# Another order of the same instructions in the attention pairs of a one-core YOCO decode step

## What is computed

```python
def stick_breaking(q, k, v, bias, q_pos, k_pos):
    z = jnp.einsum('bthd,bshd->bhts', q, k).astype(jnp.float32) * (HEAD_DIM ** -0.5) \
        + bias.astype(jnp.float32)[None, :, None, None]
    causal = k_pos[None, :] < q_pos[:, None]
    log_beta = jax.nn.log_sigmoid(z)
    log_rest = jnp.where(causal, jax.nn.log_sigmoid(-z), 0.0)
    after = lax.cumsum(log_rest, axis=3, reverse=True) - log_rest
    a = jnp.where(causal, jnp.exp(log_beta + after), 0.0)
    out = jnp.einsum('bhts,bshd->bthd', a, v.astype(jnp.float32))
```

## Time and profile before

| what | us |
|---|---|
| median of 3 runs | 2781.6 |
| the profiled execution, device time | 2782.98 |
| its span, first to last instruction | 2781.3 |
| PE busy over the span | 2681.6 (96%) |
| DVE busy | 1327.5 (48%) |
| ACT busy | 763.3 (27%) |
| POOL busy | 1008.4 (36%) |
| mean granted clock of PE | 0.978 |

### The profile page before, as it was taken

One profiled execution on the slowest core, in us unless ns is written; L12 is line 12 of the kernel. 1 busy time (PEld: TensorE's weight loads), 2 busy tenths in 40 slices (PEclk: granted clock), 3 DMA queues, 4 the chain that ended last, 5 costly groups with the idle time before them and its releaser, 6 DMA issues.

```text
span 2781.3 us, 42516 instructions
## 1 busy us (share of the span) xinstructions
PE 2681.6 (96%) x16785; PEld 2564.6 (92%) x16785; DVE 1327.5 (48%) x1343; ACT 763.3 (27%) x1096; POOL 1008.4 (36%) x534
## 2 busy tenths in 40 slices
PE   7999999999999999999999999969999999999997
PEld 6989999999999999988888888749999999999997
DVE  5244453333333333678878878782533333333335
ACT  5112110000000000367767767661200000000003
POOL 4643475667676777000000000020433333333330
PEclk8999999999999999999999999879999999999998
DMA  3111133333333333423222222222211111111111
GB/s 116 46 39 32 45 91 95 115 114 115 114 115 114 114 114 118 165 66 100 82 74 79 83 86 83 93 101 86 61 46 46 47 46 47 46 47 46 40 38 63
DMA packets 247794, 220.18 MB, mean 79 GB/s; under 512 B 12842, under 2 KB 211298, under 8 KB 247586
## 3 DMA queue, kind: packets, MB, share of 16 engines
q1 hardware_dynamic: 229090, 206.75, 23.8%
q10 hardware_dynamic: 18496, 10.49, 1.3%
HBM read 162.42 MB, written 54.77 MB: 78 GB/s over the span
## 4 chain that ended last, share of the span: by engine, by line
PE 90%; DVE 5%; ACT 2%; issue 2%; ACTq 0%; DMA 0%; SPq 0%; DVEq 0%
PE ps L762 50%; PE ps L891 18%; PE aux L1021 8%; PE ps L973 3%; PE ps L946 2%; PE ps L928 2%; PE ps L958 2%; PE aux L992 1%; DVE scratch L1686 1%; PE aux L1027 1%; DVE v_all L1714 1%; PE aux L981 1%; PE aux L1061 0%; PE ps L842 0%; DVE sp_part_odd L1841 0%
## 5 line engine op out<-in xcount | busy, mean ns | idle before, releaser
L644 POOL TENSOR_TENSOR w_hi<-w_raw,ones_col 128x1024 fp32r<-128x1024 f32 x140 | 270.9, 1935 | 821.5 <-PE ps L762 536.6
L651 POOL TENSOR_TENSOR w_lo<-w_raw,w_hi 128x1024 fp32r<-128x1024 f32 x156 | 436.0, 2795 | 12.2
L762 PE MATMUL ps<-near_hi,w_hi 128*128 128x352 f32 x1632 | 357.7, 327 | 15.7 <-DVE near_lo L1673 12.1
L762 PE MATMUL ps<-near_lo,w_hi 128*128 128x352 f32 x1632 | 354.5, 325 | 0.0
L762 PE MATMUL ps<-near_hi,w_lo 128*128 128x352 f32 x1632 | 352.5, 324 | 0.0
L762 PEld LDWEIGHTS ps<-near_hi,w_hi 128*128 128x128 f32 x1632 | 279.3, 190 | 20.0 <-issue 12.0
L762 PE MATMUL ps<-in_hi,w_hi 128*128 128x352 f32 x1320 | 286.9, 325 | 3.7 <-issue 3.7
L1800 DVE TENSOR_TENSOR h<-h,ps 128x1056 f32<-128x1056 f32 x160 | 200.1, 1251 | 188.0 <-PE ps L891 187.8
L762 PE MATMUL ps<-in_lo,w_hi 128*128 128x352 f32 x1320 | 285.5, 324 | 0.0
L762 PE MATMUL ps<-in_hi,w_lo 128*128 128x352 f32 x1320 | 284.3, 323 | 0.0
L718 POOL TENSOR_TENSOR in_lo<-o_back,in_hi 128x1056 fp32r<-128x1056 f32 x7 | 18.1, 2589 | 732.6 <-ACT in_hi L1254 732.6
(11 more groups left out here) (229 smaller groups left out, 4373.6 us busy)
## 6 DMA issues: line engine op xcount, KB each, us to landing
w_raw<-in_w_gate_dram SPq DMA_DIRECT2D x44, 512.0 KB, 4.4
w_raw<-in_w_up_dram SPq DMA_DIRECT2D x44, 512.0 KB, 4.0
w_raw<-in_w_down_dram SPq DMA_DIRECT2D x44, 512.0 KB, 3.8
kept_hi<-pre_hi SPq DMA_DIRECT2D x64, 256.0 KB, 2.1
kept_lo<-pre_lo SPq DMA_DIRECT2D x64, 256.0 KB, 2.7
w_hi<-kept_hi SPq DMA_DIRECT2D x32, 512.0 KB, 3.7
w_lo<-kept_lo SPq DMA_DIRECT2D x32, 512.0 KB, 4.6
w_raw<-in_a_w_in_dram SPq DMA_DIRECT2D x16, 512.0 KB, 3.9
```

What stands on the lines that cost most here:

```text
L644: gp.tensor_tensor(hi, raw, one, ALU.mult).then_inc(w_hi_done, 1)
L651: gp.tensor_tensor(lo, raw, as32(hi), ALU.subtract).then_inc(w_ready, 1)
L762: last = mm(out[:, c, 0:CH], w[:, ks], x[:, k, c * CH:c * CH + CH], start=(k == 0 and n == 0), stop=(k == KT - 1 and n == 2))
```

## The change

In the four functions `pair` the calls stand in another order. No call is added or dropped, and X_ORDER is unchanged; AUX_LAST and X_LAST only name lists that were written out before. The core of the diff, from the first chunk on PE to the last:

```diff
@@ SP @@
                 if more:
-                    for n in (1, 2):
-                        slab(r + n, r_of + n, (r_of + n) % 2, chunk_done, 9 * p + 3 + 3 * n)
+                    slab(r + 1, r_of + 1, (r_of + 1) % 2, chunk_done, 9 * p + 6)
+                if more:
                     v_pages(p + 1, p + 1)
+                if more:
+                    slab(r + 2, r_of + 2, (r_of + 2) % 2, chunk_done, 9 * p + 9)
@@ PE, head of the pair @@
                 if past:
-                    values(q, o, 9)
+                    take_later(q, o, 10)
                 if more:
                     x_turn(p, c, ("c", 0), more)
                 if past:
+                    values(q, o, 9)
                     carry(q, o, 10)
                 if now:
+                    sample_start(p, c)
+                    x_turn(p, c, ("p", 0), more)
                     scores(p, c, 1)
-                    x_turn(p, c, ("p", 0), more)
...
+                    sample_scores(p, c, 0)
+                    x_turn(p, c, ("p", 1), more)
                     carry(p, c, 0)
                     scores(p, c, 3)
-                    x_turn(p, c, ("p", 1), more)
@@ PE, steps 6 to 11 @@
                 if now:
                     take_later(p, c, 6)
+                    scores(p, c, 8)
                     values(p, c, 5)
-                    scores(p, c, 8)
+                    sample_later(p, c)
                     carry(p, c, 6)
+                    scores(p, c, 9)
+                    take_later(p, c, 7)
+                    values(p, c, 6)
+                    sample_values(p, c)
+                    scores(p, c, 10)
                 if more:
                     x_turn(p, c, ("c", 7), more)
...
+                if more:
+                    x_turn(p, c, ("c", 8), more)
+                if now:
                     take_later(p, c, 9)
-                    scores(p, c, 11)
+                    values(p, c, 8)
                 if more:
                     x_turn(p, c, ("v", 1), more)
                 if now:
-                    values(p, c, 8)
+                    sample_turned(p, c)
                     carry(p, c, 9)
-                    sample_values(p, c)
                 if more:
                     x_turn(p, c, ("v", 2), more)
-                if now:
-                    take_later(p, c, 10)
-                    sample_turned(p, c)
@@ ACT, head @@
                 if now:
                     act.wait_ge(bias_done, p + 1)
+                    biased(p, c, 0)
+                    v_high(p, 1)
                 if past:
                     weights(q, o, 10)
                 if now:
-                    biased(p, c, 0)
+                    turned(p, c, ("p", 0), more)
                     exp_part(p, c, 0)
@@ ACT, end @@
                 if now:
+                    exp_part(p, c, 11)
                     weights(p, c, 9)
-                    sample_rows(p)
-                if more:
-                    turned(p, c, ("v", 2), more)
-                if now:
-                    exp_part(p, c, 11)
                     log_part(p, c, 11)
@@ DVE, steps 6 and 7 @@
                     logits(p, c, 5)
                     softplus(p, c, 6)
+                    capped(p, c, 7)
                     softplus_high(p, c, 6)
+                    a_low(p, c, 5)
+                    sample_capped(p)
                     softplus_low(p, c, 6)
-                    a_low(p, c, 5)
-                    capped(p, c, 7)
-                    sample_capped(p)
...
+                    softplus(p, c, 7)
+                    sample_softplus(p)
                     logits(p, c, 6)
@@ DVE, end of the pair @@
                     a_low(p, c, 8)
+                    softplus_high(p, c, 10)
+                    out(p, 1)
+                if more:
+                    chunk_evicted(p, c, 8)
+                if now:
                     logits(p, c, 9)
-                    out(p, 1)
-                    softplus(p, c, 10)
-                    softplus_high(p, c, 10)
                     softplus_low(p, c, 10)
```

More of the change, by code:

```diff
@@ L1000, in x_turn @@
             def x_turn(p, c, item, more):
-                order = X_ORDER if more else [x for x in X_ORDER if x[0] == "p"]
+                order = X_ORDER if more else X_LAST
                 at = order.index(item)
@@ L1114, in pair @@
                 if now:
+                    scores(p, c, 4)
+                    carry(p, c, 1)
+                    x_turn(p, c, ("p", 2), more)
+                    values(p, c, 1)
                     take_later(p, c, 2)
[L1116 to L1120, removed]
                 if more:
@@ L1123, in pair @@
                 if now:
-                    take_later(p, c, 3)
+                    carry(p, c, 2)
+                    scores(p, c, 5)
                 if more:
@@ L1127, in pair @@
                 if now:
-                    scores(p, c, 5)
+                    take_later(p, c, 3)
                     values(p, c, 2)
-                    carry(p, c, 3)
                 if more:
@@ L1156, in pair @@
                 if now:
-                    take_later(p, c, 7)
+                    take_later(p, c, 8)
+                    values(p, c, 7)
                 if more:
@@ L1160, in pair @@
                 if now:
-                    values(p, c, 6)
-                    scores(p, c, 9)
+                    scores(p, c, 11)
+                    carry(p, c, 8)
                 if more:
@@ L1574, in pair @@
                     weights(p, c, 5)
+                if more:
+                    k_high(p, c, 5)
+                if now:
                     exp_part(p, c, 7)
@@ L2016, in pair @@
                     softplus(p, c, 6)
+                    capped(p, c, 7)
                     softplus_high(p, c, 6)
+                    a_low(p, c, 5)
+                    sample_capped(p)
                     softplus_low(p, c, 6)
-                    a_low(p, c, 5)
-                    capped(p, c, 7)
-                    sample_capped(p)
+                    softplus(p, c, 7)
+                    sample_softplus(p)
+                    logits(p, c, 6)
+                    softplus_high(p, c, 7)
+                    softplus_low(p, c, 7)
+                    capped(p, c, 8)
+                    a_low(p, c, 6)
+                    logits(p, c, 7)
+                if more:
+                    k_low(p, c, 3)
+                    chunk_evicted(p, c, 6)
+                if now:
+                    softplus(p, c, 8)
+                    capped(p, c, 9)
+                    softplus_high(p, c, 8)
+                    a_low(p, c, 7)
                 if more:
```

172 lines of the change are left out of this document (75 added, 97 removed).

## The result

The changed kernel took 2764.8 us (median of 4 runs, 2762.3 to 2766.0), the kernel before 2780.7 us beside it (4 runs, 2777.9 to 2782.3). The ratio is 0.9945, with a 95% interval of 0.9931 to 0.9958: faster by 15.9 us, where 11.6 were forecast. The forecast was 2770.0 us in a range of 2763 to 2780, so the time lies in the range, 2 us from its fast end.

The account below looks back on a forecast made before the run. PE was taken to set the pace in pairs 0 to 6, the ring of waits PE, ACT, DVE in pair 7. -5.1 - 0.9 - 0.4 - 0.9 - 4.3 = -11.6 us on the median 2781.6 gave 2770.0 us, range 2763 to 2780.

Parts of the forecast that it names:

- What goes in pairs 0 to 6: PE's waits for out (-5.1 us) and before the K page transposes (-0.9), and part of pair 0's K page copy wait (-0.4).
- out, K pages, pair 0 and take_later(10): Terms for pairs 0 to 6: -5.1, -0.9, -0.4, and -0.9 us for take_later(10) moving over the border into the next pair.
- The walk: Hand schedule, 0.1 us per hop: a pair closes after 82.5 us without PE waits; pair 7's values(11) comes 4.3 us earlier.
- The loop jumps: The loop's two jumps stay, with ACT's own pause starting later: 0, bounds -1 and +3 us each.
- rival C: ACT's late pause at each of the two loop jumps reaches PE, 3 us each: 2776.0 us; chance 0.12.
- Pair 7: Last pair: K page round, scores and softplus moved ahead bring the projection earlier; -4.3 us, bounds +3 and -12.
- A: Pair 7 gains nothing, as POOL and the out wait put DVE back: 2774.3 us; chance 0.20.
- D: New wait between c6 and c7 in every pair: 2777.0 us at one microsecond, 2787.5 from 2.5 us; chance 0.16.
- B: Clock stays up in pair 7 and half of its 18.1 us of waits goes: 2763.3 us; chance 0.10.
- the bound of -12: Pair 7's far bound: the four microseconds, and half of the 18.1 us of PE waits.

Follow-up runs that it names:

- e6: Changed kernel with DVE's out(p, 1) put back behind chunk_evicted(8) and logits(9) in all pairs; 2784.57 us, ratio to before 1.0017.
- e3: Kernel before with DVE's out(p, 1) one step earlier, ahead of logits(9); 2778.03 us, ratio 0.9991.
- e7: Kernel before with POOL's subtraction for in_lo doing 32 of its 1056 columns; 2774.03 us.
- e1: New order in pairs 0 to 6, the order of the kernel before in pair 7 and the tail; 2770.99 us, ratio to before 0.9964.
- e2: Order of the kernel before in pairs 0 to 6, the new one in pair 7 and the tail; 2776.26 us, ratio to before 0.9982.
- e4: Changed kernel with the loop over pairs 1 to 6 written out on SP, PE, ACT and DVE; 2754.6 us, ratio to before 0.9904.
- e12: The kernel before run again with nothing edited, for a second profile; 2778.12 us.
- e11: The changed kernel run again with nothing edited, for a second profile; 2764.68 us.
- e8: Changed kernel with POOL's subtraction for in_lo doing 32 of its 1056 columns; 2761.94 us.
- e9: Changed kernel with DVE's out(p, 1) ahead of softplus(10), a_low(8) and softplus_high(10) in pair 7 alone; 2764.18 us.

## Why the prediction was right, and where its sizes were off

**What goes in pairs 0 to 6** was right. All twelve waits are gone, and e6 shows what holds out's away: its place ahead of c8's eviction. The term was out, K pages, pair 0 and take_later(10): -7.3 us. Measured were -10.5 us between the first two profiles. Over all executions of unedited pairs 0 to 6 (four old: 595.38, 592.31, 593.32, 592.19; six new: 584.92, 582.4, 584.55, 584.5, 582.11, 580.31) the means are 593.3 and 583.1 us, so -10.2. Of the parts, the wait for the K page copy in pair 0 went whole, 0.7 us where half was charged.

**The term that was too small** is what a pair without a jump gains. It rests on a floor: "so an order of the same instructions can win only what PE waits there". I took the busy 82.86 us for the least that the pair's matmuls can take, and predicted 82.8 to 83.0 for a pair without a jump. It is 82.10, with the same 572 matmuls. The walk's 82.5 us was nearer, and I set its difference down to the error of the walk. Part of the difference is that a wait costs more than its idle time: from the start of the v1 transposes to values(8), with 0.72 us of idle in it, 1.22 us passed, and without a wait the same transposes are over after 0.35; ahead of the K pages the mask matmuls and their wait of 0.2 took 0.44 us, and 0.1 without. So the two waits were worth 1.2 us a pair and not the 0.86 that the waits view gave them. The other 0.4 us, of 1.64 in all, are steps next to which something else now stands, by the time from each step's start to the next one's: values are 0.6 us shorter in the new order, scores, the K page transposes and the sample's own steps 0.2 each, while carry, take_later and the chunks are 0.6 us longer together. No run isolates those; that they come from the neighbours is an argument, not shown. e3 warns against adding waits up: half a microsecond of idle taken away brought 0.3.

**The loop jumps** were charged at 0, with bounds of -1 and +3 each. Five executions of the old order (e3 and e7 among them) show pairs with a jump 3.6 to 6.1 us longer than those without, 4.7 in the mean of ten. Six of the new order show 4.8 to 6.6 us, 5.9 in the mean of twelve. So a loss of rival C's kind came, 1.2 us a jump instead of 3, 2.4 us in all, but not by C's chain: PE has no wait for ACT behind a jump in the new order. PE itself stands 3.19 to 3.90 us at a jump in the new order (3.56 in the mean of twelve) and 2.81 to 3.46 in the old (3.15 in the mean of ten); that is 0.4 of the 1.2. The rest is the clock: behind a jump it was low for some 7 us in eight of the twelve and in three of the ten, and for some 3 us or not at all in the others. Among jumps with a low stretch of the same length the orders are 0.6 to 0.7 us apart. Why PE stands longer, and whether the order has to do with the longer stretches, no run shows. Seven times 1.64 us, 0.9 for take_later(10) and the 0.7 us of the K page copy in pair 0 make 13.1; less 2.4 it is 10.7. The 10.2 measured are a little less, since in three of the six new executions, and in none of the four old ones, the clock was low for 3 us in pair 0's first chunk, and pair 0 took some 1.5 us longer.

**Pair 7** was forecast at -4.3 us. The profiles of the unedited kernels and of e1, e2 and e4 give 105.56, 103.52, 106.85 for the old order and 98.57, 102.21, 101.01, 103.33 for the new: means of 105.3 and 101.3, so -4.0; the medians of e1 and e2 give 4 to 6. The size was right, but the place was not. The walk gained it all ahead of take_later(3), at 32.2 instead of 36.4. It starts at 34.0 and 36.8 us in the two profiles of the changed kernel, and at 36.4 and 33.8 in those of before: no difference beyond the clock's. That is the step of the walk that failed. The gain comes behind it:

| from take_later(3) to the projection | us (granted clock) |
|---|---|
| old order: before, e12, e1 | 69.2 (0.71), 69.7 (0.72), 69.9 (0.74) |
| new order: changed, e11, e2, e4 | 64.6 (0.76), 65.4 (0.79), 68.2 (0.73), 68.9 (0.72) |
| POOL's work cut short: e7 (old), e8 (new) | 64.1 (0.74), 63.5 (0.74) |

At a clock of 0.71 to 0.74 the new order is ahead by some 1 us only. The other 3 to 4 us of two of its executions stand beside a higher clock, and which of the two brings about the other no run shows. PE's idle time in pair 7 didn't fall either (28.6, 28.3 and 31.2 us in the old order, 28.7, 30.4, 25.9 and 29.3 in the new), so the gain isn't one of shorter waits in sum. POOL is a second part: e7 and e8 give it some 3 us of the gain, and I had set that to nothing with the sentence "so I charge some 2 us each in the new walk too". The seven pieces stretched DVE by 8.4 to 10.7 us in sum, and not by 14. That a gain in a place where none came and a gain that I had put at nothing are of like size is luck.

**The rivals.** A (pair 7 gains nothing) and D (a new wait between c6 and c7) didn't come: in the changed kernel PE has no wait at all in pairs 1 to 6 but the jumps. Had D's kind of chain come, e6 shows that its price would have been above its length. Of B, the clock in pair 7 was 0.76 in one profile, but 0.60 and 0.79 in the two parts (first 32 us and the rest) of e11, with 0.79 and 0.72 in those of e12 for the old order. Over the whole pair it was 0.70, 0.74 and 0.75 in the old order and 0.76, 0.73, 0.70 and 0.73 in the new, so it moves from execution to execution more than from order to order. The measured time is next to B's 2763.3, but not by B's way: pair 7 gained 4 us and not 11. (B's 11 was said to be half of 18.1, which is 9; the bound of -12 doesn't come out of its two parts, 4 and 9, either.) The Trainium skill, "TensorE: Matmul & The Clock Gate", Part 1, has the array fall back when idle: e6 agrees in five of seven pairs, where the clock fell to 0.5 at or behind a pause of 2.17 us; in the other two the same pause left it at 1.00.

## What to carry to other kernels

The waits view gives a wait its idle time only; read also the time from the start of the group in front of it to the waiting step, against the same group where nothing waits, and don't call the busy time a floor. An order that leaves a wait with its chain (eviction, logits, out) behind PE's own last step pays for it with more than its length, since the clock may fall. Where the clock moves by itself, as in a pair that is bound by a ring of waits, one profile can't size an edit of 4 us: take a second execution of each kernel first, and set the granted clock beside every length. Before an edit that is to take a wait away, look for the other inputs that the waiting step needs: in e9 one of them left 3.26 of the 4.6 us standing.

## What the runs showed of the hardware

A pause of PE of 2.17 us came with some 3 us at the lower level of the granted clock in five of seven pairs, and with none in two; the pauses of 0.72 us in the old order came with none in seven. Each jump of this loop costs 3.6 to 6.6 us, of which PE's standing still is 2.8 to 3.9 us and most of the rest the lower clock behind it; writing three turns out took 10.2 us off the whole (e4), though two of its pairs were 0.7 and 1.0 us over the others. A POOL subtraction on 128x1056 took 2.77 us in the mean, and a DVE product on 128x768 took 2.08 us beside it instead of 0.95.
